# Cached-attention stage of a hybrid decoder step: key blocks turned on VectorE, scores in eight array tiles of 32 rows, units of 1024 keys in one unrolled chain

## The reference, cut to what matters

```python
s_past = einsum('bthc,blc->bhtl', q_lat, ckv_past) + einsum('bthr,blr->bhtl', q_pe, kpe_past)   # * SM_SCALE
s_new  = the same over the 8 new keys, causal
p      = softmax(concatenate([s_past, s_new], axis=-1))
o      = einsum('bhtl,blc->bthc', p_past, ckv_past) + einsum('bhtl,blc->bthc', p_new, ckv_new)
v      = einsum('bthc,chv->bthv', o, w_uv)          # then a gate and the output projection
```

## Time and profile before

| | us |
|---|---|
| median of 3 runs | 1920.43 (1918.05 to 1922.9) |
| span of the profiled execution | 1918.3 |
| median of the runs less the span | 2.1 |
| PE busy in the profiled execution | 1617.1 |
| DVE busy | 796.3 |
| ACT busy | 627.4 |
| POOL busy | 223.0 |
| end of `decode_attention` in the profiled execution | 1323.8 |

### The profile page before, as it was taken

The page is one execution under the profiler, slowest core; times in us unless marked ns, Lnnn a source line. Parts: engine busy times, 40 slices in busy tenths (PEclk is TensorE's granted clock), DMA queues, the critical chain, the costliest instruction groups (busy, mean ns, idle before and its releaser), DMA issues. The chain is left out here.

```text
span 1918.3 us, 26899 instructions
## 1 busy us (share of the span) xinstructions
PE 1617.1 (84%) x10091; PEld 1274.6 (66%) x10091; DVE 796.3 (42%) x1403; ACT 627.4 (33%) x1022; POOL 223.0 (12%) x219
## 2 busy tenths in 40 slices
PE   4779996688889798599898998998996999870497
PEld 1379995577777677466555565655875999870285
DVE  1240003364645537255444454544226541239633
ACT  3231212142333324233333332333433232355232
POOL 0000000000000000222222222220121000006121
PEclk7779997799989899699999999998998999995699
DMA  9821100110100000525253245222322111100322
GB/s 333 299 56 45 44 22 24 57 28 1 27 0 27 0 0 0 243 110 220 111 201 143 115 201 217 113 110 80 118 72 64 44 44 33 44 1 0 123 88 77
DMA packets 80578, 169.42 MB, mean 88 GB/s; under 512 B 9941, under 2 KB 51803, under 8 KB 76410
## 3 DMA queue, kind: packets, MB, share of 16 engines
q1 hardware_dynamic: 71290, 84.49, 13.4%
q0 software_dynamic: 9216, 83.89, 10.9%
HBM read 157.91 MB, written 10.45 MB: 88 GB/s over the span
## 5 line engine op out<-in xcount | busy, mean ns | idle before, releaser
L80 PE MATMUL bank<-in_x_hi,in_w_hi 128*128 128x272 f32 x992 | 289.8, 292 | 19.9 <-DVE in_x_lo L413 19.8
L82 PE MATMUL bank<-in_x_hi,in_w_lo 128*128 128x272 f32 x992 | 288.8, 291 | 0.0
L81 PE MATMUL bank<-in_x_lo,in_w_hi 128*128 128x272 f32 x992 | 287.4, 290 | 0.0
L80 PEld LDWEIGHTS bank<-in_x_hi,in_w_hi 128*128 128x128 f32 x992 | 188.6, 190 | 20.5 <-issue 19.8
L81 PEld LDWEIGHTS bank<-in_x_lo,in_w_hi 128*128 128x128 f32 x992 | 188.9, 190 | 0.0
L82 PEld LDWEIGHTS bank<-in_x_hi,in_w_lo 128*128 128x128 f32 x992 | 188.4, 190 | 0.0
L1164 PE MATMUL bank<-c_ident,ckv_pages 128*128 128x128 f32 x1024 | 143.0, 286 | 12.4 <-DMA ckv_pages<-in_cache_ckv,page_parts 12.4
L1040 ACT ACTIVATE k_T<-bank 128x512 f32<-128x512 f32 x192 | 114.3, 598 | 109.8 <-PE bank L1164 109.8
L1164 PEld LDWEIGHTS bank<-c_ident,ckv_pages 128*128 128x128 f32 x1024 | 119.5, 147 | 35.8 <-issue 23.1
L403 DVE TENSOR_TENSOR in_w_lo<-in_w_raw,in_w_hi 128x1024 fp32r<-128x1024 f32 x31 | 37.9, 1224 | 239.2 <-ACT in_w_hi L355 239.1
L1142 PE MATMUL bank<-k_T,q_pair 128*64 128x512 f32 x512 | 124.5, 607 | 0.0
(11 more groups left out here) (272 smaller groups left out, 2950.4 us busy)
## 6 DMA issues: line engine op xcount, KB each, us to landing
u_T<-in_w_ada SPq DMA_DIRECT2D x12, 2048.0 KB, 14.3
in_w_raw<-in_r_w_in SPq DMA_DIRECT2D x16, 512.0 KB, 3.9
in_w_raw<-in_a_w_in SPq DMA_DIRECT2D x15, 512.0 KB, 4.0
x_tiles<-in_x_prompt SPq DMA_DIRECT2D x8, 512.0 KB, 9.3
out_w_raw<-in_a_w_o SPq DMA_DIRECT2D x8, 512.0 KB, 3.6
out_x_in<-in_x_prompt SPq DMA_DIRECT2D x8, 512.0 KB, 4.0
x_mid<-out_x_new SPq DMA_DIRECT2D x8, 512.0 KB, 2.9
u_T<-in_r_w_o SPq DMA_DIRECT2D x8, 512.0 KB, 8.4
```

The costliest lines, as they stand in the source:

```text
L80: pe.matmul(out, w_hi, x_hi, start=start, stop=False)
L81: pe.matmul(out, w_hi, x_lo, start=False, stop=False)
L82: return pe.matmul(out, w_lo, x_hi, start=False, stop=stop)
```

## The change

`decode_attention` is written anew.

- **Units.** GP is 8 now, so a partition holds 8 keys of a page group. The work is cut into 32 units, eight per pair; a unit is 1024 keys of each of two sequences. No register loops: the 32 units are one unrolled chain, which does not stop between pairs. The new tokens of all pairs are done once, ahead of the chain (L1121 to L1134).
- **Loads.** Four slots of 2.62 MB; POOL only issues the four indirect DMAs of a unit (L1001) when the values of the unit four before are done. Rows are 8 KB of `ckv` and 2 KB of `kpe`.
- **Turning keys.** DVE does it: `turn(u, c)` (L1054), five transposes of 32x32 blocks, each instruction 128x1024, from SBUF to SBUF. PE's transposes of keys, the copies out of PSUM and POOL's reorder are gone. A 32x32 block transpose leaves 32 keys of each group of 32 partitions with their dimensions along those partitions, so a matmul over 32 rows of the array is wanted.
- **Scores.** For each of 10 blocks of 32 dimensions (8 of `ckv`, 2 of `kpe`) PE issues 8 matmuls of 64 columns x 256 keys (L1149), one for each of 4 row groups of 32 and each of 2 column halves, into banks 0 to 3: 80 matmuls of the program a unit. The queries stand in `q_rep`, replicated to the four row groups by 24 DMAs per pair on SP (L976, L980), the first two pairs at the start of the stage.
- **Softmax and values.** Maximum over 1024 (L1059, L1062), exponentials over 1024 on ACT (L1018), 8 transposes of the probabilities (L1159), two copies of 128x512, now on ACT (L1029), 16 matmuls of 64x256 for the values (L1170), accumulation on DVE (L1069, L1074).
- **Elsewhere.** `prompt_attention` writes `qpe` without padding: one memset and two DVE copies per pair go.

The core of the diff:

```diff
-GP = 16
+GP = 8
...
-    NPAIR, CHUNKS, SLOTS = NB // 2, PAGES // 4, 2
+    PAIRS, PER, J, SLOTS = NB // 2, GROUPS, PAGE // PPP, 4
+    UNITS, BLOCKS, STEPS = PAIRS * PER, (KVL + ROPE) // 32, (KVL + ROPE) // 64
...
+                for u in range(UNITS):
+                    slot = u % SLOTS
+                    if u >= SLOTS:
+                        pool.wait_ge(pv_done, u - SLOTS + 1)
+                    for s in range(2):
+                        at = a["parts"][:, 2 * u + s:2 * u + s + 1]
+                        for dst, name in ((ckv, "cache_ckv"), (kpe_raw, "cache_kpe")):
+                            pool.indirect_dma_start(dst[:, slot, J * s:J * s + J, :].rearrange("p j c -> p (j c)"), None,
...
+                def turn(u, c):
...
+                    if c == 0:
+                        dve.wait_ge(raw_in[slot], 64 * (u // SLOTS + 1))
+                        if u >= 2:
+                            dve.wait_ge(s_done, u - 1)
+                    src = ckv[:, slot, :, 64 * c:64 * c + 64] if c < 4 else kpe_raw[:, slot, :, :]
+                    dve.transpose(keys_of(u, 2 * c, 2).rearrange("p b (j r) -> p b j r", r=32),
+                                  src.rearrange("p j (b r) -> p b j r", r=32)).then_inc(kt_d, 1)
...
+                for u in range(UNITS):
+                    maximum(u)
+                    if u + 1 < UNITS:
+                        turn(u + 1, 3)
+                        turn(u + 1, 4)
+                    if u:
+                        accumulate(u - 1)
+                    if u + 2 < UNITS:
+                        for c in range(3):
+                            turn(u + 2, c)
...
+                def scores(u):
+                    pr = u // PER
+                    if u % PER == 0:
+                        pe.wait_ge(q_in[pr % 2], 16 * 24 * (pr // 2 + 1))
+                    for b in range(BLOCKS):
+                        if b % 2 == 0:
+                            pe.wait_ge(kt_d, STEPS * u + b // 2 + 1)
+                        for quad in range(4):
+                            rows = slice(32 * quad, 32 * quad + 32)
+                            for s in range(2):
+                                mm = pe.matmul(bank[HALF * s:HALF * s + HALF, quad, 0:KEYS], q_rep[rows, pr % 2, b, s, :],
+                                               keys_of(u, b, 1)[rows, 0, KEYS * s:KEYS * s + KEYS], start=(b == 0), stop=(b == BLOCKS - 1),
+                                               tile_position=(32 * quad, HALF * s))
+                    mm.then_inc(s_done, 1)
...
+                scores(0)
+                for u in range(UNITS):
+                    turn(u)
+                    if u + 1 < UNITS:
+                        scores(u + 1)
+                    if u % PER == 0 and u:
+                        turn_out(u // PER - 1)
+                    values(u)
```

More of the change, by code:

```diff
@@ L961, in decode_attention @@
[L961 to L965, removed]
+        ckv = sb("ckv_pages", [P, SLOTS, 2 * J, KVL])
@@ L1027, in _ @@
[L1027 to L1041 removed]
+                                                    bass.IndirectOffsetOnAxis(at, 0)).then_inc(raw_in[slot], 16)
@@ new lines, in _ @@
+                        rows, b = slice(HALF * s, HALF * s + HALF), 2 * pr + s
+                        out, at = bank[rows, NEW_BANK, NTOK * pr:NTOK * pr + NTOK], slice(NTOK * b, NTOK * b + NTOK)
+                        for c in range(VC):
+                            pe.matmul(out, a["qlat"][:, c, b, :], u_T[:, QC + c, NP + NTOK * b:NP + NTOK * b + NTOK],
+                                      start=(c == 0), stop=False, tile_position=(0, HALF * s))
+                        mm = pe.matmul(out, a["qpe"][:, b, :], a["kpe_s"][0:ROPE, at], start=False, stop=True,
+                                       tile_position=(0, HALF * s))
@@ new lines, in _ @@
+                mm.then_inc(n_scored, 1)
+                pe.wait_ge(n_exp, PAIRS)
+                for pr in range(PAIRS):
+                    mm = pe.transpose(bank[0:NTOK, NEW_BANK, P * pr:P * pr + P], p_new[:, pr, :], k["ident"][:])
+                mm.then_inc(n_turned, 1)
+                pe.wait_ge(n_kept, 1)
+                pe.wait_ge(new_in, 16)
+                for pr in range(PAIRS):
+                    for s in range(2):
+                        mm = pe.matmul(bank[HALF * s:HALF * s + HALF, PT_BANK + pr // 2, KVL * (pr % 2):KVL * (pr % 2) + KVL],
+                                       pn_T[:, pr, HALF * s:HALF * s + HALF], ckv_new[:, 2 * pr + s, :], start=True, stop=True,
+                                       tile_position=(0, HALF * s))
@@ new lines, in _ @@
+                mm.then_inc(n_valued, 1)
+                def scores(u):
[5 more added lines that the diff above has]
+                            pe.wait_ge(kt_d, STEPS * u + b // 2 + 1)
+                        for quad in range(4):
+                            rows = slice(32 * quad, 32 * quad + 32)
[4 more added lines that the diff above has]
+                    mm.then_inc(s_done, 1)
@@ new lines, in turn, with values @@
+                def turn(u):
+                    pe.wait_ge(e_done, u + 1)
+                    if u == 0:
+                        pe.wait_ge(n_done, 1)
+                    for j in range(J):
+                        mm = pe.transpose(bank[:, PT_BANK + j // 4, P * (j % 4):P * (j % 4) + P], prob[u % 2][:, j, :], k["ident"][:])
+                        if j % 4 == 3:
+                            mm.then_inc(pt_ps, 1)
+                def values(u):
+                    if u:
+                        pe.wait_ge(o_done, u)
+                    for j in range(J):
+                        if j % 4 == 0:
+                            pe.wait_ge(pt_sb, 2 * u + j // 4 + 1)
+                        for s in range(2):
+                            mm = pe.matmul(bank[HALF * s:HALF * s + HALF, O_BANK, 0:KVL], probT[:, j, HALF * s:HALF * s + HALF],
+                                           ckv[:, u % SLOTS, J * s + j, :], start=(j == 0), stop=(j == J - 1),
+                                           tile_position=(0, HALF * s))
+                    mm.then_inc(pv_done, 1)
```

387 lines of the change are left out of this document (143 added, 244 removed).

## The result

The changed kernel takes 1859.57 us (1858.57 to 1860.99, 4 runs), where the kernel before took 1920.38 beside it: a ratio of 0.9688, 95% interval 0.9675 to 0.9702. It is faster, but the forecast was 1692 with a range that ended at 1830, so most of the expected gain did not come. The profiled execution has a span of 1858.3 us, where the sum of the prediction gave 1690.4: 168 us are missing.

The account below looks back on a forecast made before the run. PE was taken to bound decode_attention; 9.0 us per unit, 30 units (270 us) plus start and tail end the stage at 1095.9 instead of 1323.8. That -227.9 gives 1690.4 profiled, 1692 us as median; range 1675 to 1830.

Parts of the forecast that it names:

- I price it at nothing, with up to 1.5 us a unit as the upper bound: Loads in the unit chain: 2.62 MB take 6.2 us at 420 GB/s, under the unit's 9.0, so no cost.
- The start: Stage start: first transposes at 790, first maximum at 800.4; the 24 query-replicating DMAs beside the first load cost nothing.
- Scores in eight tiles: PE's scores per unit: 20 groups of 256 columns at 0.215 us, 4.30 us if all eight tiles run side by side.
- The unit: PE per 1024 keys: values 3.44, turning probabilities 0.9, scores 4.30, shape changes 0.4; sum 9.0 us.
- DVE's 7.6 us: DVE's work per unit: five transposes 5.7 us plus maximum, update and accumulations; under PE's 9.0, so DVE waits for PE.
- the transposes' 1.22: Each DVE transpose of 128x1024 at 1.22 us, the ordinary pace per element; covered by PE up to 1.5 us.
- The tail: Stage end after the 30 units: softmax, turn and copies, values, last accumulation, output and the present 7.8; 17 us.
- Rival 3: PE's scores run four tiles at a time or PE is fed too slowly: 8.6 us, unit 13.3, 1825 us; chance 0.12.
- two forms, 1825 and 1870: Scores four-wide or fed at half pace, 8.6 us: 1825; at a 62 ns floor per matmul, 9.9 us: about 1870, chance 0.03.
- Rival 1: Later loads or hand-overs: POOL's wait, four issues and landing exceed the lead; unit up to 10.5 us, up to 1740; chance 0.14.

Follow-up runs that it names:

- kernel released earlier: Against the shifted kernel: POOL's loads are released by the seventh of ten score blocks, not the scores' end; 1751.04 us, ratio to the kernel before 0.9126.
- short rows: Against the changed kernel: from unit 4 on, the same four indirect DMAs from POOL fetch rows of 64 bytes; 1875.7 us in one run.
- plain loads: Against the changed kernel: from unit 4 on, SP loads the same bytes by four plain DMAs from consecutive pages, POOL issues nothing; 1754.2 us in one run.
- busy POOL: Against the kernel with plain loads: POOL does twenty additions of 64 elements in each unit; 1749.8 us in one run.
- kernel with the queries first: Against the changed kernel: POOL awaits the first pair's replicated queries before loading units 1 to 3, second pair's replicated after first scores; 1864.84 us, ratio 0.9698.
- shifted kernel: Against the changed kernel: POOL starts a unit's loads when scores end, DVE turns the whole next unit behind the maximum; 1765.16 us, ratio to the kernel before 0.919.

## Why the prediction was wrong

- **The step that failed** is "I price it at nothing, with up to 1.5 us a unit as the upper bound" for the loads. It looked at bytes, landing times and slots, and these held: from 830 to 1230 us DVE waits for no load, and none in the kernel released earlier either, with units of 10.5 us on average. It did not look at what POOL's issuing does to the engine that is the bound. That costs 3.7 us a unit, and the clock's answer to it 1.4 more on average (14.2 against 12.8), 5.1 in place of at most 1.5: 28 units x (14.2 - 9.0) = 146 us. That the issuing is the cause is shown by the kernel without reloads (stutter gone), with short rows (it stays), with plain loads (gone) and with a busy POOL (gone).
- **The start** was mis-sized: "SP's 24 replicating DMAs for a pair lie beside the first load ... nothing". They lay behind 10.5 MB of loads, and the first scores waited for them until 811.4, where unit 0 was turned at 797.74. That is 13.6 of the 17 us; 2.0 are the first transpose (791.99, forecast 790), and the rest is mostly the first scores, 5.93 us at a clock that began at 0.50. The kernel with the queries first shows the order of the transfers as the reason (795.6), and that the time is not won by that alone.
- **Scores in eight tiles** were right: 4.30 us for the streams, 4.57 measured with the end of the last, wherever POOL doesn't issue. The Trainium skill, "TensorE: Matmul & The Clock Gate", section "Wait — 56ns, not 53.3ns?", has a floor of about 62 ns per matmul without hardware decoding. It doesn't show in this trace: 160 records in 4.57 us are at most 29 ns each.
- **The unit** was right: 9.0 forecast, 9.13 measured without loads. So were DVE's 7.6 us and the transposes' 1.22, as the groups of the kernel after show; rows of the same kind are in the earlier trace rows.

```profile
L1054 DVE STREAM_TRANSPOSE k_T<-ckv_pages 128x1024 f32<-128x1024 f32 x64 | 75.7, 1221 | 0.0
```

- **The tail** was right: 17 us forecast, 17.7 measured from the last maximum's start (1243.29) to the last instruction's end (1261.04).
- **Rival 3**, "PE is fed too slowly", named the right symptom, but as a constant pace of feeding, which is not what happens: full pace for 1.1 us, five records at a time while POOL issues, full pace again. Its two forms, 1825 and 1870, lie around the measured 1860, and the range took in only the first; that the time fell between them is chance. Its sign, scores over 6 us with PE busy all along, came half true: they last 8.2 to 11.1 us in the three units above, with gaps. Rival 1 looked in the right place (POOL's four issues) for another effect.

The rows of before could have warned only in part. POOL issued the same four DMAs per group there, and PE wasn't hurt: a window of the kernel before around one such set of issues is

```profile
833.00:839.00 6.00, 6.00 (x40) 3.67 (x40) 2.82 (x5) 1.81 (x4) 4.64 (x7) 1.00 0.62 208
```

PE is busy for 6.00 of 6.00 us with 40 records. The new scores want 160 records in 4.30 us, 37 each microsecond. The prediction weighed that density against the densest row, but not together with what stood beside it.

**What stays open** is by which path POOL's issuing holds back PE's instructions and its signals. The gaps are named "issue", and no experiment here looked behind that name. The loading of the long unrolled program is not it: the kernel without reloads loads as much code (71 packets, 1.16 MB in the queue "q8 instruction" on both pages) and has no stutter, and during 16 of the 28 stutters of the changed kernel the trace has no such packet. Whether plain DMAs issued by POOL would do the same wasn't run: SP's kernel changed the engine and the kind of DMA together. How much of the last 1.3 us per unit (10.5 on average against 9.13) could be won by another moment of release was not tried, nor were loads of the real pages by SP with page numbers in registers.

## What to carry to other kernels

When a change makes the bounding engine's instructions many and short, list what the other engines issue at that moment, not only what they compute or move: here four indirect DMAs per unit, hidden before, cost 5 us a unit. A few units at the end of a chain, where one of the streams has run out, are a free experiment; here the last two, at 9.13 us, pointed at the loads before any experiment did. And if a stall can't be removed, move its cause to where the engine works in long instructions: the same issuing beside the values cost them almost nothing (gaps of 2.0 us in all in the shifted kernel), and this, with the turns moved behind the maximum, took the kernel from 1860 to 1751 us.

## What the runs showed of the hardware that was not expected

- Indirect DMAs issued from POOL hold back PE's instructions: in the changed kernel from 1.75 us after the first issue's start to about 1 us after the last one's end, dense scores get five or six records per 0.75 to 1.46 us. Rows of 64 bytes do it as much as rows of 8 KB (units of 14.8 and 14.2 us); four plain DMAs from SP (scores of 4.57 us), or 5.8 us of additions on POOL, don't.
- On PE it shows almost only in the short, dense instructions. Values (32 records in 3.67 us) and transposes (8 in 1.09) beside the same issues lose nothing in most units of the shifted kernel; over its 28 units from 830 to 1130 us the gaps named "issue" before values add up to 2.0 us, and to 18.8 before scores. But in the kernel released earlier the semaphore update of the scores' end came 1.6 us late beside them, and DVE and ACT with it.
- A stutter of 3.6 us, with 24 records in it, was followed by some three microseconds of dense work at a granted clock of 0.50 in the unit at 1000.56, and by none in the one at 987.74; with two issues in place of four the clock stayed at 1.00 from 900 to 1100 us.
